# Dilation-16 key scores of the cached keys by GpSimd and VectorE, in a hybrid decoder step on one core

## The reference

```python
for g, (w, d) in enumerate(A_GROUPS):          # (128,1), (512,4), (2048,16)
    nk = w // d + 1
    dist = jnp.arange(nk) * d
    idx = buf_lens[g] + t0 + jnp.arange(qb)[:, None] - dist[None, :]
    kg = jnp.take(ext_k[g], idx, axis=1)       # keys: cache, then new ones
    vg = jnp.take(ext_v[g], idx, axis=1)
    s = (jnp.einsum('bqhd,bqkhd->bhqk', qblk[:, :, g], kg) * scale
         - slopes[g] * dist)
    lse = jax.nn.logsumexp(s, axis=-1)
    outs.append(jnp.einsum('bhqk,bqkhd->bqhd', jnp.exp(s - lse[..., None]), vg))
```

## Time and profile before

| | |
|---|---|
| median of 3 runs | 1072.98 us |
| lowest, highest | 1071.91, 1078.2 us |
| profiled execution, its own time | 1073.26 us |
| its span | 1071.4 us |
| PE busy | 999.7 us, 93% |
| DVE, ACT, POOL busy | 539.9, 380.3, 151.2 us |
| DMA | 219.51 MB, mean 205 GB/s |

### The profile page before, as it was taken

One profiled execution on the slowest core, in us unless ns is written; L12 is line 12 of the kernel. 1 busy time (PEld: TensorE's weight loads), 2 busy tenths in 40 slices (PEclk: granted clock), 3 DMA queues, 4 the chain that ended last, 5 costly groups with the idle time before them and its releaser, 6 DMA issues.

```text
span 1071.4 us, 21575 instructions
## 1 busy us (share of the span) xinstructions
PE 999.7 (93%) x7796; PEld 926.7 (86%) x7796; DVE 539.9 (50%) x1017; ACT 380.3 (35%) x605; POOL 151.2 (14%) x149
## 2 busy tenths in 40 slices
PE   5999999999999999999989989999988999999892
PEld 5999999999999999778877777878757999999892
DVE  4246335433633454566656755675675433224338
ACT  4035213422431344345425442633454334333100
POOL 0001010101101012232312231322210000000003
PEclk8999999999999999999999999999988999999997
DMA  8775674767556564365638454643680888776602
GB/s 284 247 258 192 229 255 168 255 234 260 184 198 208 206 229 168 130 227 207 203 109 277 154 184 141 243 167 130 207 281 20 281 286 297 256 264 232 216 21 88
DMA packets 137317, 219.51 MB, mean 205 GB/s; under 512 B 7936, under 2 KB 102784, under 8 KB 135552
## 3 DMA queue, kind: packets, MB, share of 16 engines
q1 hardware_dynamic: 132704, 205.77, 56.5%
q0 software_dynamic: 3920, 10.89, 3.0%
q10 hardware_dynamic: 656, 2.36, 0.6%
HBM read 206.40 MB, written 99.88 MB: 286 GB/s over the span
## 4 chain that ended last, share of the span: by engine, by line
PE 84%; DVE 9%; ACT 3%; issue 2%; DMA 1%; DVEq 0%; ACTq 0%; SPq 0%; POOL 0%; POOLq 0%
PE bank L685 18%; PE bank L687 18%; PE bank L686 18%; PE bank L680 8%; PE bank L715 4%; PE bank L958 4%; PE bank L919 3%; DVE part_l L1574 3%; PE bank L772 2%; PE bank L794 2%; PE bank L994 1%; PE bank L1003 1%; PE bank L936 1%; ACT part_h L1256 1%; DMA xn<-in_x_prompt_dram 1%
## 5 line engine op out<-in xcount | busy, mean ns | idle before, releaser
L685 PE MATMUL bank<-xh,wh 128*128 128x288 f32 x640 | 193.1, 302 | 0.4 <-PE bank L1091 0.4
L685 PE MATMUL bank<-wh,xh 128*128 128x256 f32 x640 | 188.1, 294 | 3.5 <-DVE wl L1368 3.0
L687 PE MATMUL bank<-xh,wl 128*128 128x288 f32 x640 | 189.3, 296 | 0.0
L686 PE MATMUL bank<-xl,wh 128*128 128x288 f32 x640 | 189.2, 296 | 0.0
L686 PE MATMUL bank<-wl,xh 128*128 128x256 f32 x640 | 183.2, 286 | 0.0
L687 PE MATMUL bank<-wh,xl 128*128 128x256 f32 x640 | 183.1, 286 | 0.0
L685 PEld LDWEIGHTS bank<-wh,xh 128*128 128x128 f32 x640 | 125.3, 196 | 6.3 <-issue 3.4
L1132 ACT ACTIVATE wh<-raw 128x1024 fp32r<-128x1024 f32 (+1 forms) x104 | 101.2, 1018 | 80.1 <-PE bank L715 69.8
L686 PEld LDWEIGHTS bank<-wl,xh 128*128 128x128 f32 x640 | 125.2, 196 | 1.4
L687 PEld LDWEIGHTS bank<-wh,xl 128*128 128x128 f32 x640 | 124.8, 195 | 0.0
L685 PEld LDWEIGHTS bank<-xh,wh 128*128 128x128 f32 x640 | 121.0, 189 | 1.7 <-issue 1.4
(11 more groups left out here) (208 smaller groups left out, 1844.6 us busy)
## 6 DMA issues: line engine op xcount, KB each, us to landing
cslot<-in_cache_kv_w_dram SPq DMA_DIRECT2D x48, 1024.0 KB, 5.9
out_dram<-in_cache_kv_w_dram SPq DMA_DIRECT2D x20, 2040.0 KB, 10.4
raw<-in_w_in_dram SPq DMA_DIRECT2D x128, 256.0 KB
out_dram<-in_cache_kv_w_dram SPq DMA_DIRECT2D x24, 1020.0 KB, 9.5
out_dram<-in_cache_kv_w_dram SPq DMA_DIRECT2D x20, 504.0 KB, 5.2
raw<-in_w_in_dram SPq DMA_DIRECT2D x16, 512.0 KB
out_dram<-in_cache_kv_w_dram SPq DMA_DIRECT2D x24, 252.0 KB, 3.2
out_dram<-kv POOLq DMA_DIRECT2D x16, 256.0 KB, 3.3
```

Source lines behind the costliest of these rows:

```text
L685: pe.matmul(out, lhs[0](k), rhs[0](k), start=(k == 0), stop=False)
L686: pe.matmul(out, lhs[0](k), rhs[1](k), start=False, stop=False)
L687: last = pe.matmul(out, lhs[1](k), rhs[0](k), start=False, stop=(k == n - 1))
```

## The change

**Scores of group 2.** The eight key tiles of group 2 leave the retention stage, which keeps five tiles (KTILES). Instead, in each attention head h, ACT loads that head's cached keys of group 2 for all eight batches into one buffer, far: 128 partitions are (query q, batch b, half n), each with 64 keys of 128. The load is `far_keys(h)`: eight DMAs, one for each q, each to 16 partitions with 1,024 runs of 512 bytes (512 KB), issued by ACT between next_high(0) and next_high(1). It first waits for the sums of the head before. DVE copies the head's sample queries twice (qdup), PE turns them after unit 15, ACT copies the turn into qrow. POOL multiplies far by qrow in eight pieces of 128x1024, DVE sums each piece over its 128 columns (`far_sum`) and POOL stores the sums in DRAM (fscr). In the retention stage SP reads them back for two batches at a time (`far_scores`) and `rows(x)` adds the penalties. far_free and far_summed guard the buffers.

**Retention stage.** The two lows of POOL go to DVE, one chunk between rows(1) and normalise_rows(1), one at value tile 9 of the second batch; ACT's highs of these move too. Value units 1 and 2 and cached_probs(0) stand before the turns of the rotated queries, and the sample's state work is set at value tiles 3 to 7. Keys use cslot 0 alone, values all three, slots 1 and 2 being loaded ahead.

**Copies.** In the attention stage the caches of three batches are copied, not five; batch 4's follows in the retention stage, batch 3's in stage D behind each of the last three w_o chunks that SP issues (680 rows of 4 KB and two smaller pieces each). Batches 5 to 7 stay in the gates' stage. The score buffer and pt are each split into two (1024 and 1280 wide).

```diff
+            def far_keys(h):
+                act.wait_ge(far_summed, h * FAR_PIECES + FAR_PIECES)
+                settle(act)
+                src = caches[2].rearrange("b (n m q) c h e -> q (b n) m c (h e)", q=16, n=2)
+                for q in range(DEC_T):
+                    act.dma_start(far[q * 16:(q + 1) * 16, :, :], src[q, :, :, 0, bass.ds(h * DH, DH)])\
+                        .then_inc(far_in, 16)
...
                 next_high(0)
+                far_keys(h)
                 next_high(1)
                 group(0, kt[:, 0, :], SEQ)
                 next_high(2)
                 group(2, kt[:, 2, :], SEQ)
                 next_high(3)
+                act.wait_ge(far_turned, h + 1)
+                act.activation(qrow[:, :], bank[2][:, P:2 * P], ACT.Copy).then_inc(far_row, 1)
...
             with pool.Fori(0, H) as h:
                 store_kv(h, 0)
+                pool.wait_ge(far_row, h + 1)
+                for m in range(0, 64, FAR_PIECE):
+                    if m == 0:
+                        pool.wait_ge(far_in, h * 128 + 128)
+                    a = far[:, m:m + FAR_PIECE, :]
+                    tt(a, a, qrow[:, :].rearrange("p (a e) -> p a e", a=1).to_broadcast([P, FAR_PIECE, DH]),
+                       ALU.mult).then_inc(far_prod, 1)
                 store_kv(h, 1)
+                pool.wait_ge(far_summed, h * FAR_PIECES + 2 * FAR_PIECES)
+                pool.dma_start(fscr[bass.ds(h, 1), :, :].rearrange("h p m -> p (h m)"), fsum[:, :]).then_inc(far_out, 16)
+                pool.wait_ge(far_out, h * 16 + 16)
+                pool.sem_inc(far_free, 1)
...
+                def far_sum(n):
+                    dve.wait_ge(far_prod, h * FAR_PIECES + (n + 1))
+                    dve.tensor_reduce(fsum[:, n * FAR_PIECE:(n + 1) * FAR_PIECE],
+                                      far[:, n * FAR_PIECE:(n + 1) * FAR_PIECE, :], AX.X, ALU.add).then_inc(far_summed, 1)
...
                 cached_scores(0)
+                value_unit(1)
+                value_unit(2)
+                cached_probs(0)
                 pe.wait_ge(rot_done, r + 1)
...
+                for b in range(D_COPY_B, A_COPY_B - 1):
+                    rows(2, b, (n - 1) * 680, 680)
+                    rows(1, b, (n - 1) * 168, 168)
+                    rows(0, b, (n - 1) * 40, 40)
```

More of the change, by code:

```diff
@@ L66 @@
 B_UNITS = 10
-A_TG, B_TG = 14, 26
+A_TG, B_TG = 14, 10
 U_B = H * A_UNITS
@@ L473, in values @@
                     tiles = SLOTS[slot]
-                    load_tiles(b, 1, slot, tiles, PARTS + tiles[1])
+                    load_tiles(b, 1, slot, tiles, (PARTS if slot == 0 else KTILES) + tiles[1])
                     if slot == 0:
@@ L637, in retention_head @@
                     .then_inc(sc_stored, 16)
-                if not last:
-                    for s in range(2):
-                        pool.wait_ge(w_high, r * (2 * B_CH) + (2 * C0_B + 6 + s + 1))
-                        tt(wl[1][:, s * HW:(s + 1) * HW], wraw[s], wh[1][:, s * HW:(s + 1) * HW].bitcast(F32),
-                           ALU.subtract).then_inc(w_low, 1)
                 pool.wait_ge(sc_stored, r * 16 + 16)
@@ L836, in attention_head @@
                     q2_za_unit(u)
+                    if u == 15:
+                        pe.wait_ge(unit_free, h * A_UNITS + (3 + 15))
+                        pe.wait_ge(o_read, h * QBLK + 1)
+                        turn(bank[2][:, P:2 * P], qdup[:, :]).then_inc(far_turned, 1)
                 group_read(2)
@@ L1244, in used_b, with keys @@
                     return lambda: act.wait_ge(unit_done, r * B_UNITS + (UD + U_B + n))
-                def keys(x, between):
-                    for j in range(TILES):
-                        for tile, work in between:
-                            if j == tile:
-                                work()
+                def keys(x):
+                    for j in range(KTILES):
                         act.wait_ge(part_used, r * (2 * PARTS) + (PARTS * x + (1 if j < 3 else j - 1)))
                         settle(act)
-                        act.wait_ge(tg_done, r * B_TG + (TG_B + 13 * x + j + 1))
+                        act.wait_ge(tg_done, r * B_TG + (TG_B + KTILES * x + j + 1))
                         act.activation(part_h[j % 3][:, :], bank[2 + j % 2][:, :], ACT.Copy).then_inc(part_high, 1)
@@ L1308, in retention_head @@
                     queries(r + 1, 0)
-                values(1, 3, VTILES)
+                values(1, 3, 6)
+                if not last:
+                    high(r * B_CH + (C0_B + 3), 1, used_b(10))
+                values(1, 6, VTILES)
                 output_lows(1)
@@ L1712, in retention_head @@
                 values(0)
-                lows(0, 0, 2, TILES)
+                lows(0, 0, 2, KTILES)
+                rows(0)
+                values(1)
+                normalise_rows(0)
+                lows(0, 1, 0, 3)
+                values(2)
+                probs(0)
                 dve.wait_ge(hcon_in, r * 16 + 16)
@@ L1731, in retention_head @@
                    qdec.to_broadcast([P, QBLK, P]), ALU.mult).then_inc(rt_free[1], 1)
-                values(2)
-                probs(0)
-                lows(0, 1, 0, 3)
+                values(3)
+                b = group(2)
+                tt(atts[:, :], b[0:NS, 0:NS], const("dmats", NS)[:, bass.ds(r * NS, NS)], ALU.mult).then_inc(rt_free[0], 1)
+                lows(0, 1, 3, 6)
                 sample_output()
-                for n in range(4):
-                    sample_states(n)
-                lows(0, 1, 3, 6)
-                values(3)
-                lows(0, 1, 6, 10)
+                lows(0, 1, 6, 8)
+                sample_states(0)
+                sample_states(1)
+                lows(0, 1, 8, 10)
+                sample_states(2)
+                sample_states(3)
+                lows(0, 1, 10, 12)
                 values(4)
-                lows(0, 1, 10, VTILES)
+                lows(0, 1, 12, VTILES)
                 attention()
@@ L1750, in retention_head @@
                 chain(1)
-                lows(1, 0, 4, TILES)
+                lows(1, 0, 4, KTILES)
                 rows(1)
+                low(C0_C if last else r * B_CH + (C0_B + 2), 0)
                 normalise_rows(1)
@@ L1761, in retention_head @@
                 next_projected(2)
-                lows(1, 1, 7, 11)
+                lows(1, 1, 7, 9)
+                if not last:
+                    low(r * B_CH + (C0_B + 3), 1)
+                lows(1, 1, 9, 11)
                 normalise()
```

171 lines of the change are left out of this document (98 added, 73 removed).

## The result

The changed kernel takes 1084.75 us (median of 5 runs, 1084.39 to 1091.92), the kernel before on the same chips 1074.53. The ratio is 1.0099, with a 95% interval of 1.0076 to 1.0122: slower by 1.0%, 10 us. The forecast was 1112 us.

The account below looks back on a forecast made before the run. The prediction took PE's work, busy 93% of the span, and the few places where PE waits to bound the kernel. Its sum was 1073.3 - 60 + 5 + 85 + 7 + 2 = 1112 us, range 1018 to 1140.

Parts of the forecast that it names:

- The hold of ACT: Attention stage: ACT stuck issuing far loads until about 251, PE waiting 21 us a head for DVE's kv copy; +85 us.
- The new order of the retention stage: Retention stage: DVE taking POOL's weight lows, +8, and value units moved ahead of the rotated queries' turns, -6.
- The key tiles: Retention stage: 64 key tiles leave PE, which bounds that stretch, at 0.97 us each; -62 us.
- the prediction's own sign: Trace test for the tile price: wrong if a retention head shortens by other than 13 to 16 us.
- lows +8: Retention stage: DVE's low before normalise_rows(1) makes normalising late, 1.8 us in three heads, 2.4 in the last; +8 (0 to 14).
- waits -6: Retention stage: DVE's L1730 gets more time before the rotated queries' turns, saving 6 of 8.4 us of PE waits.
- Sums and products: Attention stage: DVE's sums delay normalisations by about 1.3 us a head, +5 (0 to 12); POOL's products free.
- the clock: Attention stage: PE's granted clock drops after each pause, about 1.7 us a pause; +7 us.
- rival (a): Attention stage: ACT not held, its queue taking all eight far issues at 0.56 us; 1020 us, chance 0.25.
- the likeliest case: Attention stage: ACT held while far loads move at about 100 GB/s; 1112 us, own range 1084 to 1145, chance 0.55.
- Copies, +2: Stage D: the first moved cache copy piece stands ahead of later w_o loads, +2 (0 to 8); copies elsewhere off the path.
- Rival (b): Attention stage: ACT held but loads at 292 GB/s, free at 229 to 239, mean 6.5 us a head; 1050 us, chance 0.12.

Follow-up runs that it names:

- experiment 7: The changed kernel with the retention stage's two weight lows back on POOL instead of DVE; 1095.81 us, one run.
- experiment 8: The changed kernel with the old order around the rotated queries in the retention stage, on PE, DVE and ACT; 1113.13 us, one run.
- experiment 11: The changed kernel without the loads of far, which is zeroed once at the begin; 1009.37 us, one run.
- experiment 4: The changed kernel with four of the eight far loads, for queries 0, 2, 4 and 6; 1056.73 us, one run.
- 3: The changed kernel with each far load going to all 128 partitions, same number of runs but wrong rows; 1032.81 us, one run.
- 5: The changed kernel with each far load going to all 128 partitions with right rows, eight turns for one, issues in one piece; 1027.65 us, ratio 0.955.
- experiment 6: The changed kernel with far loads to all 128 partitions, right rows, and their issues split three, three and two; 1016.1 us, ratio 0.9445.
- experiment 12: The 128-partition, split-issue kernel with moved sums and kv freed earlier, plus cache copies back where they were before the change; 1008.7 us, ratio 0.9376.
- experiment 2: The changed kernel with the eight far loads issued by POOL at the begin of each head instead of by ACT; 1150.06 us, ratio 1.0679.
- experiment 9: The 128-partition, right-row, split-issue kernel with DVE's sums moved to idle places and kv freed earlier by POOL; 1008.73 us, ratio 0.9363.

## Why the prediction was wrong

The sign was right, and ACT was held as forecast; the sum was not: forecast +39 us, measured +10 by the medians and +11 by the profiled runs. Two terms failed. The hold of ACT was priced at +85 us and measured 70. The new order of the retention stage was priced at +2 us, a loss at DVE's lows against a small gain in waits, and measured -5.5. The key tiles gave 5 us more than forecast. And the reason given for the cost of the load, the hold, is not the one that the experiments show (step 5). The steps:

**1. Key tiles, -62, measured -67.** I divided a stretch by its 13 tiles. But the turns of the first two tiles stand ahead of it, so it holds 13 score groups and 11 turns, and a tile taken out takes one of each: (12.5 - 4.1) / 8 and (12.8 - 4.6) / 8 are 1.04 us in the mean of one head's two batches, 64 of them 67. By the prediction's own sign the tile price fails too: a retention head was to shorten by 13 to 16 us, and shortened by 18.

**2. The order of the retention stage, forecast +2 (lows +8, waits -6), measured about -5.5** (the stage's -72.5 less the -67 of the tiles). This is where the prediction failed in kind. The +8 was normalising made late by DVE's low in every head. PE's waits for it are 1.9 us, once, for 0.5 before, and they are the same 1.9 where POOL makes the lows (experiment 7), so none of them comes from the low; what the lows do cost is 2.7 us of waits for wl, in two places. That POOL's lows would have cost 8.6 us more in the new order (experiment 7) was not looked at. The order around L1730, with the sample's state work, is worth 28 us, not 6 (experiment 8). I read the waits of before as if the key tiles stayed. With them out and the old order kept, PE waits 6.1 us for POOL's rotation, which it never did before, and the stage is 44.4 us shorter than before where the tiles alone are worth 67: 22.6 us are lost again. That the missing tiles had covered this work is how I read it; no run takes the tiles out and changes nothing else. The new order wins the 22.6 back and 5.5 more. The stage as a whole came out at -72.5 where I had -60.

**3. Sums and products, +5, measured 5.5** (experiment 11). The size is luck in part: the waits that it was made of, at L1460 (L1503 now), grew by 1 us only, from 1.3 to 2.3; 2.9 us are waits for vn, which PE did not have before, and 1.4 is PE's own work (384.6 for 383.2). The low at 223.65 took 4.67 us for two halves beside the products; whether the waits for vn come from it or from the sums was not tried in this order.

**4. The hold, +85, measured 70; the clock, +7, measured 8.4.** Held at about 100 GB/s is what happened: 104 GB/s, and next_high(1) 18 us late in three heads and later in the first. When the last issue returned, at 289.8, 2,799 of the load's 8,320 packets were still to move, where the prediction let ACT wait until 1,700 to 2,000 were left: 2.8 MB had moved, not 3.0. (In experiment 4 it was 2,789, in 3 and 5 2,466 and 2,585.) The rest of the size: I let the issues begin at 218, when the activations before them end, 3.7 us into the head. They begin 0.8 us into it: the first issue starts at 259.22, the activation that stands before it in the code at 260.14. And the hold was 30.6 us, not 33. That makes 16 us a head in three heads and 21.5 in the first, for 21. The clock is PE's busy time in the attention stage, 393.0 us, less the 384.6 of the run without loads, all at full clock.

**5. The reason behind the hold.** The prediction called the hold the cause and the rate its multiplier. Both cost, but the rate is the larger cause: the load at 104 GB/s keeps all DMA engines busy for some 40 us a head and delays the weights by nearly as much as the hold delays ACT. Take the hold away and 5 us come back; take the slow rate away and 52 to 57 do (experiments 3 and 5); both, 69 (experiment 6). My rival (a), no hold, was priced at 1020 us; without contention in its price that number meant nothing, since no hold gives 1080. So the held case and the case without a hold lie 5 us apart, and it is luck that the forecast of the first had the sign right without its cause: a time alone could not have told them apart.

**6. Copies, +2, measured 0** in stage D's window and in experiment 12.

In sum: -5, -7.5, +0.5, -15, +1.4 and -2 against the terms are the 27.6 us between 1112 and the profiled run's 1084.4. The range of the likeliest case began at 1084, the measured time, but that range is not what the ends of its terms add up to, which is 1070 to 1170. Rival (b) has such a slip too: its bounds, ACT free at 229 to 239, give 0 to 9 us a head, 4.5 in the middle and not 6.5.

The Trainium skill gives, in "SBUF — State Buffer", Door 1: The DMA port swizzle, 104 GB/s for a load to 16 partitions; the trace agrees, with 104. The same page, Who interferes with whom, says that a DVE instruction with two SBUF inputs contends with a GpSimd instruction that reads SBUF; the trace agrees, 5.11 us for the two halves of a low beside the products and 2.35 without them. I had weighed the first and not looked for the second, which spoke against POOL's lows beside value tiles (experiment 7).

## What to carry to other kernels

The load to few partitions was slow for everyone here: it kept every DMA engine busy at a third of the rate. So look at the partition count of each transfer before asking which queue should issue it, and turn the layout so that each DMA spans all 128, even at the price of a wider operand elsewhere (here 8 turns for 1, and 57 us less). Issues in the stream of an engine that has other work belong in portions that the queue can take, three of 1,024 pieces here. Before a transfer goes to another queue, see what it will stand beside there, at the start of the kernel too (experiment 2). When work is taken off the bounding engine, ask of each wait behind it what had covered it: the tiles that go are a price of their own, and the order must be made new around the gap.

## What the runs showed that I had not expected

Contention was worst where ACT was not held: POOL took the eight issues in 6 us, and ACT then waited 42 us for weights; the whole was 75 us slower than before, half of that at the start. Two operations with two SBUF operands each, one on DVE and one on POOL, slow each other from 1.2 to 2.6 us and from 2.36 to 3.35, and the sum looks as if only one ran at a time. From 282.96 on (experiment 9) the rest of the sixth product, the two halves of the low and the last two products, each at its undisturbed length, would end one after another at 290.7 by my estimate; they end at 290.3. In the first head of that kernel the low took all of it, 7.66 us, and the two products none, 4.74. In experiment 8 the granted clock is 0.5 from a wait of 1.3 us at 603 to 610, with waits of 1.5, 0.4 and 0.4 us in the 10 us before, then 1.0, and after a wait of 2.1 us 0.57 on average from 613 to 617. And the layout with right rows, split issues and moved sums runs at 0.936 of the kernel before: what the change was after was there, 76 us below what it got.
